# The adaLN products beside the mLSTM of a streaming encoder layer: from full-format matmuls to high and low parts in the rounded format

## The chip, the cores and the metric

The kernel runs as one program on one core of one Trainium2 chip. The metric is the time of one execution on the device, in microseconds (us). One core has five engines that run side by side and wait for each other through semaphores: TensorE (PE in the profile, its weight loads PEld), VectorE (DVE), ScalarE (ACT), GpSimd (POOL) and SyncE (SP), which here only issues DMAs.

## The reference

One layer of a hybrid encoder, for a prompt of 2048 tokens and for a sample of 32 tokens with its states. A conditioning row c gives six rows of shift, scale and gate. The part that the change touches is the product that makes them; the mLSTM is computed at the same time as four of the six.

```python
def adaln(c, w_ada, b_ada):
    mod = jax.nn.silu(c) @ w_ada + b_ada          # (1024) @ (1024, 6144), once for the prompt, once for the sample
    return jnp.split(mod[:, None, :], 6, axis=-1)

def trunk_layer(x, c, p, ...):
    sh1, sc1, g1, sh2, sc2, g2 = adaln(c, p['w_ada'], p['b_ada'])
    h = rmsnorm(x, p['norm1_w']) * (1 + sc1) + sh1
    ... projection; mLSTM in chunks (4 heads of 128); stick-breaking attention ...
    mix = jnp.concatenate([y_a, y_b], axis=-1) @ p['w_out']
    x = x + g1 * mix
    h2 = rmsnorm(x, p['norm2_w']) * (1 + sc2) + sh2
    f_out, conv_new = conv_ffn(h2, conv_state, p['w_up'], p['w_conv'], p['b_conv'], p['w_down'])
    x = x + g2 * f_out
```

## The kernel before

The program has four phases with a barrier of all engines behind each: `front` (the first two adaLN rows, the norm and the combined projection), `attention` (stick-breaking), `mlstm_output` and `ffn`. The change is in `mlstm_output` alone.

`mlstm_output` goes over 17 chunks of 128 tokens, 16 of the prompt and one of the sample. Each engine has its own program in the order in which it is written; nothing is scheduled by a planner. TensorE and VectorE go by slots (`chunks`): slot t works on chunk t and prepares chunk t + 1. TensorE's slot is `turn(t+1)` (the decay exponents into `mpD`, then twelve transposes into `mpT`), `numerator(t)`, `scores(t+1)`, `update(t)` and, last, `modulate(t)`: the product of the activated conditioning (`silu_c`, 128 x 2 for each of eight blocks of the 1024 rows) with 256 columns of `w_ada`, into the PSUM bank `mpm`. There are 16 such products, one in each of the slots 0 to 15. VectorE's slot is `prepare(t+1)` (`mqw`, `mVU`, `mDM` and two copies `mT`), `modulation_row(t-1)` (adds the product to the bias row in `mmod_rows`), `decay(t)` (`mC<-mC,decay`), `weigh(t+1)` (`mSW`) and `finish(t)` (the new memory `mC`, four small operations on `mdn`, and the output tile `mH`). ScalarE scales k (`mks`), copies v (`mVI`), copies a transposed tile (`mT`), takes the exponential (`mWX`), and rounds a piece of the output projection's weights (`w_out_high`). GpSimd issues the DMA that stores `mH`, then subtracts to get the low part of that piece (`w_out_low`).

SyncE issues the loads in the order of the chunks: three tiles `mx`, two small rows, then, when the product two chunks earlier is through with the buffer, 1 MB of `w_ada` into `mwa` (two buffers), and 256 KB of `w_out`. So SyncE waits for a product in each slot and has the next chunk's `mx` queued behind it.

Two number formats matter. A float32 matmul runs as two records for each one that is written; a matmul on tiles of the rounded format (`F32R`, fp32r in the trace) as one. Elsewhere the kernel already works with pairs: a high part, which is the value rounded (ScalarE's copy into an `F32R` tile), and a low part, the value less the high part, with three of the four products of the pairs added up. The mLSTM's own products and the adaLN products are in plain float32.

Behind the last slot come the first two norms of the output stage (`first_norms`, on VectorE), the sample's chunk, and then the output projection, which TensorE carries.

Of the kernel before, what the change touches and what calls it, by code (L numbers as in the profile page):

```python
# [6 lines left out]
F32 = mybir.dt.float32  # L7
# [5 lines left out]
P = 128  # L13
# [1006 lines left out]
def mlstm_output(k, c, gc, dec):  # L1020
# [16 lines left out]
    wo_high, wo_low = k.sems("w_out_high", "w_out_low")  # L1037
    bias_in, mod_psum, mod_ready, mod_turned, mod_row, mod_stored, plus_one, scale_ready = k.sems(
        "bias_loaded", "mod_summed", "mod_ready", "mod_turned", "mod_row_ready", "mod_stored", "scale_plus_one", "scale_ready")
    NM = 6 * KD - NMOD  # L1040
# [11 lines left out]
    with ExitStack() as s:  # L1052
# [11 lines left out]
        with ExitStack() as over:  # L1064
# [9 lines left out]
            yT = psum(nc, over, "eyT", [P, D])  # L1074
        wa = sbuf(nc, s, "mwa", [P, 2, KD, 2 * P])
        mod_rows = sbuf(nc, s, "mmod_rows", [2, NM * P])
# [12 lines left out]
        dn = sbuf(nc, s, "mdn", [P, 4, MH])  # L1089
        H = sbuf(nc, s, "mH", [P, 2, MH, MD])  # L1090
        pT = psum(nc, s, "mpT", [P, 3, W5])
        pN = psum(nc, s, "mpN", [P, 2, W5])
# [34 lines left out]
        def _(sp):  # L1127
# [18 lines left out]
            def body(t, u, r, first):  # L1146
# [9 lines left out]
                if not (isinstance(t, int) and t == NPT):  # L1156
                    if not first:
                        sp.wait_ge(mod_psum, t - 1)
                    sp.dma_start(wa[:, u], d["w_ada"].rearrange("(k p) n -> p k n", p=P)
                                 [:, :, bass.ds(t * 2 * P + NMOD * P, 2 * P)]).then_inc(w_in[u], 16)  # L1160
                    sp.dma_start(wL_plain[:, bass.ds(t, 1)].rearrange("p o n -> p (o n)"),
                                 d["w_out"].rearrange("(k p) n -> k p n", p=P)[bass.ds(r, 1), :, u * W5:(u + 1) * W5]
                                 .rearrange("o p n -> (o p) n")).then_inc(wo_in[u], 16)
# [25 lines left out]
        def _(pool):  # L1189
            nc.gpsimd.memset(LG[:], 1.0).then_inc(ones_ready, 1)  # L1190
            nc.gpsimd.memset(RU[:], 1.0).then_inc(ones_ready, 1)
            nc.gpsimd.memset(VI[:], 1.0).then_inc(ones_ready, 1)
            nc.gpsimd.memset(C[0][:], 0.0).then_inc(ones_ready, 1)

            def body(t, u, r, first):
                pool.wait_ge(h_ready, t + 1)
                pool.dma_start(d["h_d"][tok(t), :], H[:, u].rearrange("p h e -> p (h e)")).then_inc(stored[u], 16)
# [24 lines left out]
        def _(act):  # L1222
# [48 lines left out]
            act.preload_act_table_set("natural_log_exp_and_others")  # L1271
            act.wait_ge(ones_ready, 4)

            def body(t, u, r, first):
# [4 lines left out]
                nc.scalar.activation(ks[:, u], x[:, u, 1], ACT.Copy, scale=MD ** -0.5).then_inc(k_scaled, 1)  # L1279
                nc.scalar.activation(VI[:, u, :, 0:MD], x[:, u, 2], ACT.Copy).then_inc(v_ready, 1)  # L1280
                act.wait_ge(turned, t + 1)
                nc.scalar.activation(T[:, u, 0], pT[:, 0].rearrange("p (h e) -> p h e", e=P), ACT.Copy).then_inc(q_taken, 1)
# [16 lines left out]
        def _(dve):  # L1299
# [124 lines left out]
            def modulation_row(t):  # L1424
                dve.wait_ge(mod_psum, t + 1)
                span = bass.ds(t * 2 * P, 2 * P)
                v.tensor_tensor(mod_rows[:, span], pm[0:2, 0:2 * P], mod_rows[:, span], ALU.add).then_inc(mod_row, 1)

# [22 lines left out]
        def _(pe):  # L1451
# [55 lines left out]
            def modulate(chunk):  # L1507
                t, u, r = chunk
                pe.wait_ge(w_in[u], 16 * r + 16)
                at_least(pe, mod_row, t)  # L1510
                for kk in range(KD):
                    mm = t_.matmul(pm[0:2, 0:2 * P], c["silu_c"][:, kk, :], wa[:, u, kk], start=(kk == 0),
                                   stop=(kk == KD - 1))
                mm.then_inc(mod_psum, 1)

# [674 lines left out]
```

## Time and profile before

| | |
|---|---|
| median of 3 runs | 3301.67 us (3301.16 to 3303.12) |
| the profiled execution's own time | 3299.27 us |
| its span in the profile | 3297.3 us |
| mean granted TensorE clock, share of full speed | 0.983 |
| busy, share of the span | PE 96%, PEld 85%, DVE 47%, ACT 33%, POOL 23% |
| chain that ended last, share of the span | PE 44%, DVE 1%, issue 1% |
| GpSimd's first instruction of `mlstm_output` | 1332.91 us from the span's start |
| TensorE's first matmul of the output projection | 1518.52 us |

The span is the time from the first to the last instruction in the profile; the execution's own time is a little longer. A time in a row counts from the span's start. A busy share says how long an engine had something running, not how long the others waited for it, and the records of TensorE overlap, so that its pace is read from one start to the next.

### The profile page before, as it was taken

The numbers are of one execution on the slowest core, as the hardware profiler recorded it, in microseconds if no ns is written. First come the engines' busy times: TensorE is split into PE (matmuls) and PEld (weight loads), VectorE is DVE, ScalarE is ACT, GpSimd is POOL, SyncE is SP. The second block draws the span as 40 slices with busy tenths as digits, with TensorE's granted clock in tenths as the row PEclk, the third lists the DMA queues.
The fourth block names the chain that finished last, engine by engine and source line by source line (L and its number), as shares of the span: only waits on it lengthen the run. The fifth ranks groups of instructions, "written<-read, shape, count | busy, mean of one in ns | idle before, by whom it ended". The sixth has DMA issues, their size and how long they took to land. (4 is left out here: it accounts for less than half of the span.)

```text
span 3297.3 us, 45305 instructions
## 1 busy us (share of the span) xinstructions
PE 3172.6 (96%) x17258; PEld 2792.8 (85%) x17258; DVE 1539.7 (47%) x1979; ACT 1075.7 (33%) x2073; POOL 773.7 (23%) x688
## 2 busy tenths in 40 slices
PE   7999999898999999899996999999999999999999
PEld 3878887677998999677885999999999998887886
DVE  2300015532898899576652534444444346324331
ACT  3611112222776777224553222212212213213110
POOL 2421113321665666111110111111111115002000
PEclk9999999999999999899997999999999999999999
DMA  5322224433522340575544111111111114444432
GB/s 189 109 72 71 71 71 139 130 109 101 140 53 53 68 87 10 184 249 205 179 150 156 52 51 34 43 51 51 51 48 29 51 51 168 170 144 151 144 120 72
DMA packets 250868, 336.08 MB, mean 102 GB/s; under 512 B 58652, under 2 KB 170840, under 8 KB 243932
## 3 DMA queue, kind: packets, MB, share of 16 engines
q1 hardware_dynamic: 234526, 284.75, 28.3%
q0 software_dynamic: 14864, 49.31, 4.5%
q8 instruction: 94, 1.54, 0.2%
q14 instruction: 52, 0.43, 0.0%
q10 hardware_dynamic: 1332, 0.06, 0.0%
HBM read 225.16 MB, written 108.89 MB: 101 GB/s over the span
## 5 line engine op out<-in xcount | busy, mean ns | idle before, releaser
L2031 PE MATMUL facc<-fh,fwH 128*128 128x416 f32 x3520 | 948.8, 350 | 25.3 <-DVE fh L1916 25.3
L2031 PEld LDWEIGHTS facc<-fh,fwH 128*128 128x128 f32 x3520 | 662.4, 188 | 33.4 <-issue 25.9
L2031 PE MATMUL facc<-fh,fwL 128*128 128x416 f32 x1760 | 622.3, 354 | 0.0
L642 PE MATMUL pacc<-pring,h1H 128*128 128x512 f32 x1360 | 445.0, 398 | 9.5 <-POOL h1L L524 5.8
L952 POOL TENSOR_TENSOR aS<-aS,aC 128x512 f32<-128x512 f32 (+3 forms) x326 | 333.8, 1030 | 191.5 <-DVE aC L914 188.8
L914 DVE TENSOR_TENSOR_SCAN aC<-aB,aC,a 128x512 f32<-128x512 f32 (+3 forms) x326 | 362.7, 1113 | 15.2 <-ACT aB L889 9.0
L1925 DVE TENSOR_SCALAR fV<-fU,fcw,fcb 128x2048 f32<-128x2048 f32 (+2 forms) x90 | 118.4, 1357 | 528.8 <-ACT fU L1799 512.3
L1797 ACT ACTIVATE fU<-facc 128x416 f32<-128x416 f32 (+1 forms) x220 | 112.9, 514 | 771.4 <-PE facc L2031 771.4
L1885 POOL TENSOR_TENSOR fwL<-fraw,fwH 128x1024 fp32r<-128x1024 f32 x44 | 132.7, 3016 | 851.9 <-ACT fwH L1788 851.9
L2031 PEld LDWEIGHTS facc<-fh,fwL 128*128 128x128 f32 x1760 | 330.9, 188 | 2.0
L2057 PE MATMUL dacc<-dfreed 128*128 128x512 f32 (+1 forms) x1380 | 321.4, 390 | 6.4 <-DVE dfreed L1972 3.7
L642 PEld LDWEIGHTS pacc<-pring,h1H 128*128 128x128 f32 x1360 | 259.6, 191 | 65.2 <-POOL h1L L524 5.9
L2057 PEld LDWEIGHTS dacc<-dfreed 128*128 128x128 f32 (+1 forms) x1380 | 248.9, 181 | 72.9 <-POOL dfreed L1898 5.3
L1010 PEld LDWEIGHTS a_out<-av,aA 128*128 128x128 f32 x2176 | 281.7, 191 | 19.1 <-issue 1.9
L1010 PE MATMUL a_out<-av,aA 128*128 128x64 f32 x2176 | 282.8, 269 | 0.0
L642 PE MATMUL pacc<-pring,h1L 128*128 128x512 f32 x680 | 268.2, 394 | 0.0
L968 PE MATMUL a_z<-ak,aq 128*128 128x512 f32 (+3 forms) x640 | 208.4, 408 | 13.1 <-DMA aq<-qk_T 13.1
L889 ACT ACTIVATE aB<-a_z 128x512 f32<-128x512 f32 (+3 forms) x326 | 174.5, 535 | 107.7 <-PE a_z L979 49.3
L642 PE MATMUL pacc<-plate,h1H 128*128 128x512 f32 x544 | 182.2, 395 | 4.9 <-POOL plate L520 4.9
L994 PE MATMUL a_x<-ident,aS 128*128 128x128 f32 x1106 | 176.1, 275 | 4.5 <-DVE aA L881 4.1
L296 ACT ACTIVATE pstage<-pacc 128x512 f32<-128x512 f32 x119 | 70.5, 594 | 323.3 <-PE pacc L642 323.2
L894 ACT ACTIVATE aS<-a_z 128x512 f32<-128x512 f32 (+3 forms) x326 | 174.7, 536 | 0.0
(275 smaller groups left out, 4207.6 us busy)
## 6 DMA issues: line engine op xcount, KB each, us to landing
proj_out<-pstage SPq DMA_DIRECT2D x119, 256.0 KB, 2.0
dfreed_plain<-act_d SPq DMA_DIRECT2D x20, 1408.0 KB, 6.3
fraw<-w_up SPq DMA_DIRECT2D x44, 512.0 KB, 5.5
act_d<-fV SPq DMA_DIRECT2D x21, 1024.0 KB
qk_T<-pturn POOLq DMA_DIRECT2D x68, 256.0 KB, 3.1
mwa<-w_ada SPq DMA_DIRECT2D x16, 1024.0 KB, 5.6
dthird_plain<-act_d SPq DMA_DIRECT2D x11, 1408.0 KB, 6.3
praw<-w_in SPq DMA_DIRECT2D x56, 256.0 KB, 2.8
```

What stands on the lines that cost most here:

```text
L642: op = mm_(acc[:, n % NB], h[:, kk, tok(t)], weight(q, w), start=(kk == 0 and part == 0), stop=(kk == KD - 1 and part == 2))
L889: nc.scalar.activation(part(B, RB, n), part(Z, NZ, n), ACT.Sigmoid, scale=-1.0).then_inc(pass_ready, 1)
L894: nc.scalar.activation(part(S, RS, n), part(Z, NZ, n), ACT.Sigmoid).then_inc(stop_ready, 1)
L914: v.tensor_tensor_scan(buf[:, a:b][:, ::-1], part(B, RB, n)[:, ::-1], nought[:, 0:width(n)], buf[:, b:b + 1], ALU.mult, ALU.add).then_inc( ...
L952: nc.gpsimd.tensor_tensor(at, at, buf[:, a + 1:b + 1], ALU.mult).then_inc(w_ready, 1)
L968: mm = nc.tensor.matmul(to, Q[:, b, half, i * P:(i + 1) * P], K[:, b, span], start=(half == 0), stop=(half == 1), skip_group_check=True)
L994: mm = nc.tensor.transpose(X[:, n % NX, j * P:(j + 1) * P], src[:, j * P:(j + 1) * P], c["ident"][:])
L1010: mm = nc.tensor.matmul(O[:, r % 2, 0:SD if kind == PROMPT else 4 * SD], weight[:, j * P:(j + 1) * P], value, start=(top(n) and j == 0), s ...
L1885: nc.gpsimd.tensor_tensor(wL[:, j], raw[:, j], wH[:, j].bitcast(F32), ALU.subtract).then_inc(w_low, 1)
L1925: v.tensor_scalar(V[:, j, at:at + width], U[:, j, u0:u0 + width], tap(0), cb[:, ft], ALU.mult, ALU.add).then_inc(first_tap, 1)
L2031: mm = nc.tensor.matmul(dst, a[:, j, kk], b[w][:, kk], start=(kk == 0 and m == 0), stop=(kk == KD - 1 and m == 2))
L2057: mm = nc.tensor.matmul(down_acc[0:w, n % 2], at[:, l, kk, 0:w], r, start=(kk == 0 and m == 0), stop=(kk == LAST and m == 2))
```

## The change

Each block of `w_ada` that has landed in `mwa` is split. ScalarE rounds it, half by half (four of eight blocks, 128 x 1024 elements each), into a new tile `mwaH`; GpSimd subtracts that from the raw values and writes the difference over them, in place, as `mwaL`. The conditioning is split once, at the start, into a stationary tile `mcHL` of 34 columns: the high part in columns 0 and 1, zeros in 2 to 31, the low part in 32 and 33. TensorE then makes two matmuls in the rounded format for each of the eight blocks: `mcHL` (34 columns) with `mwaH`, and the first two columns of `mcHL` with `mwaL`. The result stands in rows 0 and 1 and rows 32 and 33 of `mpm`, and VectorE adds both, one after the other, to the bias row. SyncE waits for the product's second half (`mod_half`) where it waited for the product (`mod_psum`).

```diff
@@ buffers and constants
-        wa = sbuf(nc, s, "mwa", [P, 2, KD, 2 * P])
+        with ExitStack() as over:
+            wa = sbuf(nc, over, "mwa", [P, 2, KD, 2 * P])
+        wa_low = sbuf(nc, s, "mwaL", [P, 2, KD, 2 * P], F32R)
+        cHL = sbuf(nc, s, "mcHL", [P, KD, 34], F32R)
+        wa_high = sbuf(nc, s, "mwaH", [P, 2, KD // 2, 2 * P], F32R)
@@ SyncE, body(t)
-                        sp.wait_ge(mod_psum, t - 1)
+                        sp.wait_ge(mod_half, 2 * t - 2)
@@ GpSimd
+            pool.wait_ge(c_set, 2)
+            nc.gpsimd.tensor_tensor(cHL[:, :, 32:34], c["silu_c"][:], cHL[:, :, 0:2].bitcast(F32), ALU.subtract).then_inc(c_set, 1)
+
+            def split_low(t, u):
+                for e in range(2):
+                    half = slice(e * KD // 2, (e + 1) * KD // 2)
+                    pool.wait_ge(wa_split, 2 * t + e + 1)
+                    nc.gpsimd.tensor_tensor(wa_low[:, u, half], wa[:, u, half], wa_high[:, e].bitcast(F32), ALU.subtract
+                                            ).then_inc(wa_done, 1)
 
             def body(t, u, r, first):
+                if not (isinstance(t, int) and t == NPT):
+                    split_low(t, u)
                 pool.wait_ge(h_ready, t + 1)
@@ ScalarE
+            nc.scalar.activation(cHL[:, :, 2:32], C[0][:].rearrange("p h m -> p (h m)")[:, 0:30 * KD]
+                                 .rearrange("p (k j) -> p k j", k=KD), ACT.Copy).then_inc(c_set, 1)
+            nc.scalar.activation(cHL[:, :, 0:2], c["silu_c"][:], ACT.Copy).then_inc(c_set, 1)
+
+            def split_high(t, u, r):
+                act.wait_ge(w_in[u], 16 * r + 16)
+                for e in range(2):
+                    at_least(act, mod_half, 2 * t + e - 1)
+                    at_least(act, wa_done, 2 * t + e - 1)
+                    nc.scalar.activation(wa_high[:, e], wa[:, u, e * KD // 2:(e + 1) * KD // 2], ACT.Copy).then_inc(wa_split, 1)
 
                 nc.scalar.activation(VI[:, u, :, 0:MD], x[:, u, 2], ACT.Copy).then_inc(v_ready, 1)
+                if not (isinstance(t, int) and t == 0):
+                    split_high(t - 1, 1 - u, r - 1 + u)
                 act.wait_ge(turned, t + 1)
@@ VectorE
             def modulation_row(t):
-                dve.wait_ge(mod_psum, t + 1)
+                dve.wait_ge(mod_half, 2 * t + 2)
                 span = bass.ds(t * 2 * P, 2 * P)
-                v.tensor_tensor(mod_rows[:, span], pm[0:2, 0:2 * P], mod_rows[:, span], ALU.add).then_inc(mod_row, 1)
+                v.tensor_tensor(mod_rows[:, span], pm[0:2, 0:2 * P], mod_rows[:, span], ALU.add).then_inc(mod_high, 1)
+                dve.wait_ge(mod_high, t + 1)
+                v.tensor_tensor(mod_rows[:, span], pm[32:34, 0:2 * P], mod_rows[:, span], ALU.add).then_inc(mod_row, 1)
@@ TensorE
             def modulate(chunk):
                 t, u, r = chunk
-                pe.wait_ge(w_in[u], 16 * r + 16)
                 at_least(pe, mod_row, t)
-                for kk in range(KD):
-                    mm = t_.matmul(pm[0:2, 0:2 * P], c["silu_c"][:, kk, :], wa[:, u, kk], start=(kk == 0),
-                                   stop=(kk == KD - 1))
-                mm.then_inc(mod_psum, 1)
+                if isinstance(t, int) and t == 0:
+                    pe.wait_ge(c_set, 3)
+                for e in range(2):
+                    pe.wait_ge(wa_done, 2 * t + e + 1)
+                    for kk in range(KD // 2):
+                        t_.matmul(pm[0:34, 0:2 * P], cHL[:, e * KD // 2 + kk, :], wa_high[:, e, kk], start=(e == 0 and kk == 0),
+                                  stop=False, skip_group_check=True)
+                        mm = t_.matmul(pm[0:2, 0:2 * P], cHL[:, e * KD // 2 + kk, 0:2], wa_low[:, u, e * KD // 2 + kk],
+                                       start=False, stop=(e == 1 and kk == KD // 2 - 1), skip_group_check=True)
+                    mm.then_inc(mod_half, 1)
```

GpSimd's program at its first two chunks, with a minus as it was and with a plus as it is. Names are tiles, `out<-in`; a row is an instruction, x2 two alike.

```order
-L1197 DMA h_d<-mH 128x512
-L1201 TENSOR_TENSOR w_out_low<-w_out_plain,w_out_high 128x512
-L1197 DMA h_d<-mH 128x512
-L1201 TENSOR_TENSOR w_out_low<-w_out_plain,w_out_high 128x512
...
+L1207 TENSOR_TENSOR mwaL<-mwa,mwaH 128x1024 x2
+L1214 DMA h_d<-mH 128x512
+L1218 TENSOR_TENSOR w_out_low<-w_out_plain,w_out_high 128x512
+L1207 TENSOR_TENSOR mwaL<-mwa,mwaH 128x1024 x2
+L1214 DMA h_d<-mH 128x512
+L1218 TENSOR_TENSOR w_out_low<-w_out_plain,w_out_high 128x512
```

Two subtractions of 128 x 1024 stand now ahead of each chunk's store of `mH`, and behind the chunk before's `w_out_low`.

ScalarE's program at the second chunk, as it was:

```order
L1279 ACTIVATE mks<-mx 128x512
L1280 ACTIVATE mVI<-mx 128x4x128
L1282 ACTIVATE mT<-mpT 128x512
L1285 ACTIVATE mWX<-mDM 128x512
L1289 ACTIVATE w_out_high<-w_out_plain 128x512
```

And as it is:

```order
+L1306 ACTIVATE mks<-mx 128x512
+L1307 ACTIVATE mVI<-mx 128x4x128
+L1299 ACTIVATE mwaH<-mwa 128x1024 x2
+L1311 ACTIVATE mT<-mpT 128x512
+L1314 ACTIVATE mWX<-mDM 128x512
+L1318 ACTIVATE w_out_high<-w_out_plain 128x512
```

The two roundings of chunk t - 1's weights stand in chunk t's body, between the copy of v and the copy of the transposed tile for which `scores` waits. TensorE's and VectorE's programs keep their order; only `modulate` and `modulation_row` are longer by the instructions of the diff.

## Rows read from the trace of the kernel before

**Rows 1.** Busy us of PE, PEld, DVE, ACT, POOL; PEclk, DMA share, GB/s.

```profile
1385.00:1395.00 10.00, 9.21 (x66) 6.66 (x65) 7.51 (x15) 2.90 (x5) 1.82 (x2) 1.00 0.75 256
1445.00:1455.00 10.00, 10.00 (x71) 7.32 (x70) 7.96 (x15) 3.17 (x6) 1.82 (x2) 1.00 0.76 257
```

**Rows 2.** TensorE in order of time, one slot; start us, us, engine, line.

```profile
1448.33 1.15 PE L1495 MATMUL mpD<-mRU,mLG 2*128 2x128 f32 x8
...
1454.45 3.62 PE L1512 MATMUL mpm<-mwa,silu_c 128*2 128x256 f32 x16
1457.99 1.15 PE L1495 MATMUL mpD<-mRU,mLG 2*128 2x128 f32 x8
```

**Rows 3.** ScalarE, GpSimd and VectorE in that slot, in order of time.

```profile
1446.40 0.69 DVE L1420 TENSOR_TENSOR mH<-mpN,mdn 128x512 f32<-128x512 f32 x1
...
1447.48 0.63 ACT L1279 ACTIVATE mks<-mx 128x512 f32<-128x512 f32 x1 [1.27 <-DMA mx<-proj_out]
...
1447.75 0.55 POOL L1197 DMA_DIRECT2D h_d<-mH  x1 [7.69 <-DVE mH L1420]
...
1448.31 1.27 POOL L1201 TENSOR_TENSOR w_out_low<-w_out_plain,w_out_high  x1
...
1448.77 1.38 DVE L1375 TENSOR_TENSOR mVU<-mVI,gate_cols 128x516 f32<-128x516 f32 x1 [0.38 <-ACT mVI L1280]
...
1452.87 0.69 DVE L1399 TENSOR_TENSOR mC<-mC,decay 128x516 f32<-128x516 f32 x1 [0.29 <-PE mpN L1542]
...
1455.35 0.16 DVE L1412 SCALAR_TENSOR_TENSOR mdn<-mdn 128x4 f32<-128x4 f32 x1
...
1456.18 0.69 DVE L1420 TENSOR_TENSOR mH<-mpN,mdn 128x512 f32<-128x512 f32 x1
```

**Rows 4.** TensorE in order of time, two products of 512 columns.

```profile
1529.90 0.40 PE L1474 MATMUL eacc<-w_out_high,eyH 128*128 128x512 f32 x1
1530.13 0.40 PE L1474 MATMUL eacc<-w_out_high,eyL 128*128 128x512 f32 x1
```

**Rows 5.** All instructions of three lines: ns min/median/max, first and last start.

```profile
L1885 POOL TENSOR_TENSOR fwL<-fraw,fwH x44: 2329/2767/3395, 1758.3 to 2729.1; 128x1024 fp32r<-128x1024 f32 x44
L524 POOL TENSOR_TENSOR h1L<-h_plain,h1H x17: 2345/2392/2404, 54.5 to 157.9; 128x1024 fp32r<-128x1024 f32 x17
L1788 ACT ACTIVATE fwH<-fraw x44: 1039/1062/1064, 1757.2 to 2727.8; 128x1024 fp32r<-128x1024 f32 x44
```

**Rows 6.** VectorE and GpSimd in the ConvFFN, in order of time.

```profile
1824.98 2.35 DVE L1929 SCALAR_TENSOR_TENSOR fV<-fU,fcw,fV 128x2048 f32<-128x2048 f32 x1
1826.19 3.40 POOL L1885 TENSOR_TENSOR fwL<-fraw,fwH 128x1024 fp32r<-128x1024 f32 x1 [7.89 <-ACT fwH L1788]
1827.24 2.40 DVE L1929 SCALAR_TENSOR_TENSOR fV<-fU,fcw,fV 128x32 f32<-128x32 f32 x1
```

**Rows 7.** First and last slots, in order of time.

```profile
1356.55 3.62 PE L1512 MATMUL mpm<-mwa,silu_c 128*2 128x256 f32 x16
...
1357.45 0.16 DVE L1412 SCALAR_TENSOR_TENSOR mdn<-mdn 128x4 f32<-128x4 f32 x1
...
1358.06 0.69 DVE L1420 TENSOR_TENSOR mH<-mpN,mdn 128x512 f32<-128x512 f32 x1
...
1360.10 1.15 PE L1495 MATMUL mpD<-mRU,mLG 2*128 2x128 f32 x8
...
1504.28 0.69 DVE L1420 TENSOR_TENSOR mH<-mpN,mdn 128x512 f32<-128x512 f32 x1
...
1506.41 0.41 DVE L1427 TENSOR_TENSOR mmod_rows<-mpm,mmod_rows 2x256 f32<-2x256 f32 x1 [1.45 <-PE mpm L1512]
...
1508.07 0.69 DVE L1310 TENSOR_TENSOR ey<-ey,ewrow 128x512 f32<-128x512 f32 x1
```

**Rows 8.** A long wait of TensorE in the projection, and the clock behind it.

```profile
516.73 1.05 PE L683 MATMUL pR<-ident,pstage 128*128 128x128 f32 x4 [2.56 <-DVE pturn L450]
518.00:520.00 2.00, 2.00 (x6) 1.61 (x5) 1.58 (x3) 1.22 (x3) 0.37 (x1) 0.50 0.83 244
```

More of the change, by code:

```diff
@@ L1037, in mlstm_output @@
     wo_high, wo_low = k.sems("w_out_high", "w_out_low")
-    bias_in, mod_psum, mod_ready, mod_turned, mod_row, mod_stored, plus_one, scale_ready = k.sems(
-        "bias_loaded", "mod_summed", "mod_ready", "mod_turned", "mod_row_ready", "mod_stored", "scale_plus_one", "scale_ready")
+    bias_in, mod_ready, mod_turned, mod_row, mod_stored, plus_one, scale_ready = k.sems(
+        "bias_loaded", "mod_ready", "mod_turned", "mod_row_ready", "mod_stored", "scale_plus_one", "scale_ready")
+    wa_split, wa_done, c_set = k.sems("w_ada_high", "w_ada_low", "c_parts_set")
+    mod_half, mod_high = k.sems("mod_half_summed", "mod_high_added")
     NM = 6 * KD - NMOD
```

## The prediction

> **What bounds the kernel now.** I read the page first: TensorE is busy 96% of the span and carries the chain that ended last, so the question is what the changed stage, the mLSTM between 1333 and 1518 us, is worth on that chain. Then the busy times of two stretches [rows 1]: at 1445 TensorE is busy throughout, at full clock, while VectorE has 8.0 of 10 us, ScalarE 3.2, GpSimd 1.8 and the DMA engines 0.76 of their time. The reader is to see that TensorE sets the pace but VectorE is close behind. Then one slot of TensorE in order of time [rows 2]: it starts at 1448.33, the product at 1454.45, the next slot at 1457.99. So a slot is 9.66 us: 6.12 for the chunk, 3.54 for the product, in 16 records of 0.221 us each. From the first whole slot's start at 1360.10 to the last product's reduction at 1506.41 [rows 7] the average is 9.75, since a few slots also wait. Last, what the other engines do in that slot [rows 3]; this decides the case, as follows.
>
> **TensorE's part.** The 16 records become 16 matmuls of 256 columns in the rounded format. No such width of that format is in this stage. Bounds: 512 columns of the same format go by 0.23 us from start to start [rows 4], half of which is 0.115; a record of the old product has 0.221 (no gain at all). The format is the one of rows 4 and only the length differs, so I take 0.115: 1.85 us for 3.54, and a slot that TensorE alone would finish in 7.97. That would be 15 x 1.7, some 26 us, were TensorE the only one to go by.
>
> **ScalarE's part.** Two copies of 128 x 1024 at 1.06 us [rows 5], 2.1 us a slot, beside 3.2 in 10. They need the product before to be through. Behind `mks` (which runs 0.85 us ahead of the slot's start [rows 3]) and the copy of v, they run from about 0.6 to 2.7 us of the slot; behind them waits the copy `mT`, whose transposes end at about 2.4. `scores` needs that copy near 4.1. So ScalarE is covered by some 0.6 us; without the cover each us would be one of the slot.
>
> **GpSimd's part, which I take to be the new bound.** Two subtractions of 128 x 1024. The same shape and formats took 2.33 at least and 2.77 in the median in the ConvFFN, and 2.39 with a spread of 0.06 in the front [rows 5]. The long ones contain waits: the one at 1826.19 took 3.40, but VectorE held it until 1827.3, and from there it is 2.33 [rows 6]. I take 2.39. With the store's 0.55 and the 1.27 of `w_out_low` [rows 3] GpSimd has 6.6 us of work in a slot, which alone would fit.
>
> It doesn't run alone, though. In the slot shown VectorE's `mVU` is given 1.38 us where its neighbours of this shape have 0.69: it starts at 1448.77 inside GpSimd's operation (1448.31 to 1449.58) and ends 0.57 after it [rows 3]. And in the ConvFFN an operation of 32 columns took 2.40, until GpSimd's ended [rows 6]. So VectorE's operations on two SBUF operands wait for GpSimd's subtraction, however small they are, and GpSimd's for theirs. In a slot there are five on VectorE: `mqw`, `mVU`, `decay`, and two small ones on `mdn`. The Trainium skill, in SBUF — State Buffer, section Who interferes with whom, says this: a VectorE instruction with two SBUF inputs and a GpSimd instruction that reads SBUF exclude each other for a whole instruction, and whichever starts first has its way; the trace agrees, with the 1.38 and the 2.40.
>
> Now the loop. GpSimd's order is: store of `mH`, `w_out_low`, first subtraction, second subtraction, then the wait for the next `mH`. VectorE comes to `decay` 4.54 into the slot (1452.87), some 4.7 with the second addition, in the middle of the first subtraction, and gets its turn between the two; its first small operation (7.0 in) falls into the second subtraction and waits for its end; behind it `mH` is queued, and for `mH` GpSimd waits. From one `mH` to the next:
> - end of `mH` (1447.09) to the store 0.66, to `w_out_low` 0.56, its length 1.27 [rows 3];
> - subtraction 2.39; `decay` between them 0.50 (the 0.57 above, less an overlap of 0.07 seen in rows 6); subtraction 2.39;
> - small operations and `mH`: 1.52 from 1455.35 to 1456.87 [rows 3], 1.30 from 1357.45 to 1358.75 [rows 7]; since a blocked operation ends about 0.1 sooner, I take the lower.
>
> That is 9.07 us for 9.75. TensorE's second half of a product starts 0.15 after the second subtraction and takes 0.92, so TensorE waits about 1.1 us between the halves, and its slot ends 0.2 before `mH` does. A rule that speaks against the change is in the GPSIMD Engine Reference of the Trainium skill, section Elementwise — side-by-side cycle accounting: a two-input operation goes at about 2.6 cycles per element. At the page's clock this estimate gives 2.2 us, and a loop of 8.7; the measured 2.39 decides.
>
> **DMA and VectorE beside it.** No transfer is added. SyncE's wait for the product keeps its place: behind it are queued the load of `mwa`, of `w_out` and the next `mx`, which lands about 8.7 us after the slot's start (1457.0 for 1448.33), 0.4 before the next slot at 9.07. So the load stays hidden, at some 0.81 of the DMA engines. The second addition costs VectorE 0.45; it stands ahead of `decay`, which waits for GpSimd anyway: nothing. The three small instructions for `mcHL` run while `mx` loads: nothing.
>
> **The sum**, on the rows of the first and last slots [rows 7]. `mH` of chunk 0 ends at 1358.75, as before. Fifteen loops of 9.07 bring chunk 15's to 1494.8; it was 1504.97. VectorE then starts the last addition at 1494.7 instead of 1506.41: 11.7 us earlier. From there to `ey<-ey,ewrow` it was 1.66. Now 0.45 is added, and `w_out_low` is asked for inside this stretch and holds the port 1.27 us: 2.9, so 1.2 is lost. Behind it everything moves with VectorE. 11.7 - 1.2 = 10.5. One more term: if `decay` comes after the second subtraction has begun, it, `weigh` and the addition to `mC` stand between that one's end and `mH`, and the loop is 1.5 longer, once, since the next starts later. In slot 1 the two are within 0.3 us; at half weight 0.8. Sum 9.7: the profiled execution's own 3299.27 becomes 3289.6, and the median, 2.4 above it, 3292.0.
>
> **Rivals.**
> - *GpSimd's subtractions don't hold up VectorE.* Then VectorE and the transposes make the loop (`mH`'s end 8.54 into the slot, `mqw` 0.6, TensorE ready 1.1 into the next: 8.2, and 0.3 of the second addition): 8.5. 15 x 0.57 and the tail's 1.2 more: 3282. Against it stand rows 3 and 6; for it only that all rows with small operands are of 32 columns, not 4.
> - *The subtraction is longer here*, as in the ConvFFN's median of 2.77: loop 9.83, 11.4 us back: 3303. The same time comes if late `mx` tiles put `mVU` behind `w_out_low` in most slots. Gain and loss meet at 2.74 us.
> - *Slower: TensorE's clock.* TensorE now waits 1.1 us in each slot. At 516.73 it had waited 2.56, and by 518 the granted clock was 0.50, the lower level of 1.2 GHz; at 1385 it waited 0.79 in ten and stayed at 1.00, 2.4 GHz [rows 8, 1]. If 1.1 us is enough, the slot's first 2.4 us take twice as long: 15 x 2.4 = 35, so 3327. It decides somewhere between waits of 0.8 and 2.6. TensorE: Matmul & The Clock Gate (the Trainium skill), What's actually happening, has the same two levels.
> - *The rounded format is no faster at 256 columns*: product 3.54, its second half 1.8 behind the second subtraction, loop about 9.6 to 9.9: 3300 to 3305.
>
> **How the numbers follow.** Forecast (3287 to 3296) 0.50; no hold-up, or a partial one (3280 to 3287), 0.14; longer subtraction, late loads or several slots out of order (3296 to 3308) 0.24; format without gain 0.03; clock, or subtractions of 2.95 and more (over 3308), 0.09. This kernel's measurement can tell about 0.2%, 6.6 us, from no change: faster is below 3295.1, slower above 3308.3. Of the forecast 0.46 of 0.50 lies below 3295.1, so faster 0.60; slower 0.11 with the far part of the longer subtractions; same 0.29. The range leaves out a tenth at either end: 3283 to 3305.
>
> **What the changed profile would show.** The old 256 records' places filled by matmuls with starts 0.11 to 0.12 apart; a wait of about 1.1 us of TensorE for GpSimd's `mwaL` in the middle of each product, at clock 1.00; `mwaL` at 2.3 to 2.5 with `decay` between the two; a small `mdn` operation of about 1 us that ends with the second; slots of 9.0 to 9.2. I am wrong if the small operation isn't held, if the slots are below 8.7, or if the wait of GpSimd isn't for `mH`.

## The result and the profile after

| | before | after |
|---|---|---|
| median | 3301.41 us (3300.24 to 3303.12, 4 runs) | 3324.04 us (3319.04 to 3327.05, 4 runs) |
| ratio of after to before | | 1.0067, 95% interval 1.0049 to 1.0084 |
| profiled execution, its span, mean clock | 3299.27, 3297.3, 0.983 | 3324.46, 3322.8, 0.975 |
| `mH` of chunk 0 to `mH` of chunk 15, end to end | 146.2 us, 9.75 a slot | 169.6 us, 11.31 a slot |

The kernel became slower by 22.6 us, where 3292.0 was forecast. The last row says where: the fifteen slots between those two ends took 23.4 us more. The rest of the span differs by 2 us. (Times of runs below come with the ratio to runs of the kernel before on the same chip; a line number is that of the kernel named.)

The windows that answer to [rows 1], of the changed kernel: busy us of PE, PEld, DVE, ACT, POOL; PEclk, DMA share, GB/s.

```profile
1385.00:1395.00 10.00, 9.87 (x81) 9.16 (x80) 8.22 (x16) 4.16 (x6) 5.20 (x4) 0.94 0.49 153
1445.00:1455.00 10.00, 8.59 (x61) 8.13 (x62) 7.84 (x13) 5.43 (x9) 6.45 (x4) 0.83 0.70 231
```

TensorE was busy throughout at 1445; now it stands idle for 1.4 of 10 us and is at half clock for a third of them. VectorE's busy time has hardly changed (it counts what an operation is held as busy), and GpSimd has 6.45 us. So no engine is full: they wait for each other, and the order in time has to show how. (PEclk is a mean over the window: 0.83 is full clock for two thirds of it and half clock for the rest.) The changed kernel's product first, TensorE in order of time:

```profile
1453.42 0.28 PE L1546 MATMUL mpm<-mwaH,mcHL 128*34 128x256 f32 x1
1453.54 0.28 PE L1548 MATMUL mpm<-mwaL,mcHL 128*2 128x256 f32 x1
1453.65 0.28 PE L1546 MATMUL mpm<-mwaH,mcHL 128*34 128x256 f32 x1
```

Starts are 0.115 us apart, as forecast, only the second comes 0.20 behind the first. From a product's first start to the next slot's it is 2.02 us where TensorE doesn't wait, for 3.54 before; 1.85 was forecast. TensorE's part is right but for those 0.17 us. Now GpSimd and VectorE of the changed kernel in two slots, each engine apart in order of time; they answer to [rows 3].

```profile
1360.60 0.59 POOL L1214 DMA_DIRECT2D h_d<-mH  x1 [5.23 <-DVE mH L1449]
1361.21 1.28 POOL L1218 TENSOR_TENSOR w_out_low<-w_out_plain,w_out_high 128x512 fp32r<-128x512 f32 x1
1362.44 4.64 POOL L1207 TENSOR_TENSOR mwaL<-mwa,mwaH 128x1024 fp32r<-128x1024 f32 x2
...
1391.58 4.67 POOL L1207 TENSOR_TENSOR mwaL<-mwa,mwaH 128x1024 fp32r<-128x1024 f32 x2
...
1360.82 6.83 DVE L1404 TENSOR_TENSOR mVU<-mVI,gate_cols 128x516 f32<-128x516 f32 x1
...
1393.29 3.53 DVE L1428 TENSOR_TENSOR mC<-mC,decay 128x516 f32<-128x516 f32 x1
1396.84 0.69 DVE L1416 TENSOR_TENSOR mSW<-mpS,mWX 128x512 f32<-128x512 f32 x1
```

The two subtractions take 4.64 and 4.67 together, 2.33 each, with nothing between them. `decay` comes at 1393.29, in the middle of the first, and ends at 1396.82, 0.57 behind the second: it was not let in between. In the other slot `mVU` comes at 1360.82, while GpSimd issues its DMA, and is held for 6.83 us: through that, `w_out_low` and both subtractions, to 0.57 behind the last. Over the stage:

```profile
L1428 DVE TENSOR_TENSOR mC<-mC,decay x15: 672/1905/3526, 1370.1 to 1523.7; 128x516 f32<-128x516 f32 x15
```

That is the group of all 15 `decay` of the prompt's chunks from the second on: ns least, median, most, against 0.69 in [rows 3]. Five of them take 3.48 to 3.53, as the one above. Six take 1.8 to 2.2: they are issued only when the second subtraction runs, like this one (GpSimd, then VectorE).

```profile
1448.06 4.66 POOL L1207 TENSOR_TENSOR mwaL<-mwa,mwaH 128x1024 fp32r<-128x1024 f32 x2
...
1451.48 1.80 DVE L1428 TENSOR_TENSOR mC<-mC,decay 128x516 f32<-128x516 f32 x1 [1.41 <-PE mpN L1578]
```

All eleven end some 0.57 behind the second subtraction. The other four take 0.67 to 0.70; three of them are in the slots with a long `mVU`. `mVU` is held 6.78 to 6.83 us three times. From one `mH` to the next it is 10.4 to 10.6 us in the eleven slots with a held `decay`, once 11.07, and 14.3, 14.5 and 13.8 in the three with the long `mVU`.

### The profile page after: what moved, and what is told of

It reads as the page before. It is cut to its first block and busy times, and to the rows that moved or that the text cites. A ratio compares the mean times of both kernels' runs of the same rounds, so it can differ in the third digit from the quotient of the medians.

```text
span 3322.8 us, 45499 instructions
## 1 busy us (share of the span) xinstructions
PE 3170.1 (95%) x17258; PEld 2817.6 (85%) x17258; DVE 1573.4 (47%) x1995; ACT 1107.3 (33%) x2107; POOL 847.4 (26%) x721
```

## The experiments

"Spacing" is the mean from one end of `mH` to the next, chunk 0 to 15; it is read in each profile in the way of the last row of the table above.

| kernel | median, us | ratio to before (95%) | spacing |
|---|---|---|---|
| `old_product_split_beside` | 3325.37 | 1.0067 (1.0045 to 1.0089) | 11.59 |
| `turns` | 3308.04 | 1.0020 (1.0009 to 1.0030) | 10.15 |
| `turn_for_decay` | 3319.00 | 1.0051 (1.0035 to 1.0066) | 10.87 |
| `free_of_port` | 3309.39 | 1.0025 (1.0015 to 1.0035) | 10.49 |
| `store_by_sync` | 3324.70 | 1.0062 (1.0047 to 1.0077) | 10.92 |
| `own_waits` | 3305.84 | 1.0008 (0.9999 to 1.0018) | 9.87 |
| `no_low` | 3299.82 | 0.9994 (0.9984 to 1.0003) | 9.75 |
| `no_low_early_loads` | 3277.84 | 0.9929 (0.9912 to 0.9946) | 8.31 |
| `before_early_loads` | 3299.19 | 0.9994 (0.9984 to 1.0004) | 9.66 |
| `own_waits_early_loads` | 3299.83 | 1.0001 (0.9991 to 1.0010) | 9.53 |
| `turns_early_loads` | 3298.06 | 0.9991 (0.9982 to 1.0001) | 9.75 |
| `turns_early_store` | 3321.84 | 1.0058 (1.0041 to 1.0074) | 10.42 |
| `all_handed_over` | 3283.35 | 0.9939 (0.9926 to 0.9953) | 8.15 |
| `before_same_moves` | 3307.57 | 1.0019 (1.0010 to 1.0028) | 9.66 |
| `handed_store_by_gpsimd` | 3281.88 | 0.9937 (0.9921 to 0.9952) | 8.46 |
| `handed_late_loads` | 3300.19 | 0.9992 (0.9983 to 1.0002) | 9.60 |
| `handed_over_tail` | 3279.91 | 0.9926 (0.9913 to 0.9940) | 8.12 |

**Is it the product, or what prepares it?** `old_product_split_beside` keeps the kernel before and its product, and adds only the roundings and the subtractions, whose results nobody uses:

```diff
+                if not (isinstance(t, int) and t == 0):
+                    split_high(t - 1, 1 - u, r - 1 + u)
...
+                if not (isinstance(t, int) and t == NPT):
+                    split_low(t, u)
```

> The kernel before, with its float32 product, and beside it ScalarE's roundings and GpSimd's subtractions, whose results nothing uses. Theory P: the loop from mH to mH is the one of the changed kernel, 10.5 us or more, time 3318 to 3328. Theory C: the product in two float32 passes keeps TensorE busy and its clock near 1.00, so the time is within 5 us of 3301.

It loses the same as the changed kernel, though its clock falls less: over the stage, 1360 to 1530 us, the mean granted clock is 0.95 in its profile and 0.88 in the changed kernel's. So the loss comes from the work beside TensorE, and neither from the new matmuls nor from a clock that would fall because they are short.

**Is it the port?** `turns` makes GpSimd wait for the two held operations:

```diff
                 for e in range(2):
                     half = slice(e * KD // 2, (e + 1) * KD // 2)
                     pool.wait_ge(wa_split, 2 * t + e + 1)
+                    pool.wait_ge(vw_ready if e == 0 else decayed, t + 2 - e)
```

> GpSimd's first subtraction of a block waits until VectorE's mVU is done and its second until VectorE's decay is done; nothing else is changed. Theory P (port kept): GpSimd keeps the shared port over operations that it has queued, so decay waits for both subtractions (3.48 us in the changed kernel) and mVU now and then for three operations (6.8 us). Then this kernel hands the port over: decay about 1 to 2 us at most, loop from mH to mH 9.1 to 9.4 for 10.6, time 3293 to 3300. Theory C (clock): TensorE's waits pull its clock to about 0.85 and that makes the slots long. TensorE still waits in the middle of each product here, so the time stays at 3312 to 3325.

16 us of the 22.6 come back, below the range of the clock theory, but above the 3293 to 3300 that I expected of the other. No `decay` takes over 1.07 us, no `mVU` over 2.25. Only the shorter slots reach 9.2, and between them stand others of 10 to 13.4.

`turn_for_decay` keeps the second of these waits alone (`if e == 1: pool.wait_ge(decayed, t + 1)`).

> The changed kernel with one wait more: GpSimd's second subtraction waits for decay (the computation is whole). It makes the order that my forecast took for granted (decay between the two subtractions). Port theory: decay is 0.7 to 1.1 us and not 3.5, the slots that were 10.54 become 9.1 to 9.3, but mVU is held as before (where GpSimd's DMA issue or w_out_low runs, 3 us and more), so the time is between turns and the changed kernel, 3308 to 3316 us. Rival, all of the loss is in mVU: 3322 to 3326 us as the changed kernel.

`decay` is down to 1.2 us at most, but `mVU` is now held for 4.0 to 4.6 us seven times, and slots alternate between 9.1 and 12.3. It gave back 5 us and not the 8 to 16 that I expected: in this order, most of the price passes to `mVU`.

`free_of_port` takes the port away from VectorE: ScalarE does `decay`, four copies with a scale, and the denominators are two operations that read PSUM.

```diff
-                v.tensor_copy(dn[:, 0].rearrange("p (b h) -> p b h", b=2), num[:, :, :, MD]).then_inc(dn_ready, 1)
...
+                v.scalar_tensor_tensor(out=pair(dn[:, 1]), in0=num[:, :, :, MD], scalar=-1.0, in1=pair(g[:, 2]), op0=ALU.mult,
+                                       op1=ALU.max).then_inc(ab_ready, 1)
...
+                v.tensor_tensor(pair(dn[:, 2]), num[:, :, :, MD], pair(dn[:, 1]), ALU.max).then_inc(fl_ready, 1)
@@ ScalarE, behind the exponential
...
+                    for h in range(MH):
+                        op = nc.scalar.activation(C[0][:, h], C[0][:, h], ACT.Copy,
+                                                  scale=dec[:, bass.ds(t - 1, 1), h:h + 1].rearrange("p o h -> p (o h)"))
+                    op.then_inc(decayed, 1)
```

> The changed kernel with decay of chunks 0 to 15 on ScalarE (four copies with a scale, behind mWX) and the denominators from PSUM in two VectorE operations with one SBUF operand each instead of three, so that of VectorE's operations only mqw and mVU can meet GpSimd at the port. Theory P: loop 8.3 to 8.9, except where mVU is caught; time 3282 to 3291. Theory C: no difference to the changed kernel beyond the shorter chain on VectorE, 3312 to 3322.

Slots of 7.9 appear, the length that TensorE alone would need, but beside 12.0, and three `mVU` of 6.8 with slots of 14 to 14.7. So the 3309.39 misses the 3282 to 3291 that I expected.

**By what rule does GpSimd keep the port?** `store_by_sync` gives the store of `mH` to SyncE (`sp.dma_start(d["h_d"]...)` behind `w_out`'s load, none on GpSimd).

> The changed kernel with only the store of mH issued by SyncE in place of GpSimd (the computation is whole). If the hold-ups of 6.8 us of mVU come about because it is issued while GpSimd's DMA issue runs and GpSimd's next three operations follow at once, they are gone or different: the three slots of 13.8 to 14.5 us shrink to about 10.6, and the time is 3310 to 3316 us. Rival, w_out_low alone holds mVU as long: no change, 3321 to 3327 us.

The time is unchanged, for two reasons that cancel. The holds of 6.8 us are gone, as expected, but eleven `mVU` of 2.84 to 2.86 took their place, and the fifteen slots took 5.8 us less in all; and from chunk 15's `mH` to the end of the span it is 7.2 us longer, which comes back below. The profile showed something else too: VectorE's `mVU` and GpSimd's pair of subtractions.

```profile
1409.10 2.85 DVE L1410 TENSOR_TENSOR mVU<-mVI,gate_cols 128x516 f32<-128x516 f32 x1
...
1408.50 5.67 POOL L1215 TENSOR_TENSOR mwaL<-mwa,mwaH 128x1024 fp32r<-128x1024 f32 x2 [4.99 <-ACT mwaH L1305]
```

Here `mVU` ends at 1411.95, inside the pair, and the pair takes 5.67 and not 4.67: VectorE was let in between. What differs is ScalarE's second rounding: here it ended at 1409.37, after the first subtraction had begun (1408.50), so that the second still had a wait unmet at that time; in the changed kernel both roundings were over at 1361.32, before the first subtraction (1362.44). `own_waits` tests just that, with waits of GpSimd for itself:

```diff
                     pool.wait_ge(wa_split, 2 * t + e + 1)
+                    at_least(pool, wo_low if e == 0 else wa_done, t if e == 0 else 2 * t + 1)
```

> The changed kernel, its computation whole, with two waits of GpSimd for itself and for nothing else: before the second subtraction it waits until its own first one is through, and before the first until its own last w_out_low is. No order between engines is set. Theory 1, GpSimd goes on with the port when its next operation has nothing left to wait for at the time it comes up, and gives it to a waiting VectorE when it has to stop for a semaphore (in store_by_sync mVU was let in after the first subtraction, 2.85 us, where the rounding of the second half ended while the first subtraction ran; in the changed kernel both roundings were through before): decay is held for one subtraction at most (1 to 2.4 us), no mVU over 2.5, loops of 9.1 to 9.4 where the loads are in time, 3304 to 3313 us, near turns. Theory 2, GpSimd has the port until its queue is empty or it waits for another engine: decay 3.5 and mVU 6.8 stay, 3320 to 3327 us.

No order between engines is set, and still 18 us come back. No `mVU` is over 2.24 and no `decay` over 2.35, one operation of GpSimd at most beside a DMA issue; pairs take 4.85 to 5.83 us. So it is the queue: GpSimd goes straight on to its next operation when that has nothing left to wait for early enough, and VectorE, though it waited first, comes behind all of them. How early is not settled. In `store_by_sync` the second rounding ended 0.87 us after the first subtraction had begun, and VectorE was let in, eleven times of eleven. In `old_product_split_beside` roundings ended 0.37 to 0.77 after the operation before had begun, in two slots, and `mVU` was held through all the same; here ScalarE, GpSimd and VectorE in one of them:

```profile
1400.65 1.99 ACT L1290 ACTIVATE mwaH<-mwa 128x1024 fp32r<-128x1024 f32 x2
...
1402.27 4.65 POOL L1202 TENSOR_TENSOR mwaH<-mwa,mwaH 128x1024 fp32r<-128x1024 f32 x2
...
1400.88 6.61 DVE L1396 TENSOR_TENSOR mVU<-mVI,gate_cols 128x516 f32<-128x516 f32 x1 [0.38 <-ACT mVI L1298]
```

The Trainium skill, in SBUF — State Buffer, section Who interferes with whom, has it that the port pair shared by VectorE and GpSimd is an exclusive lock, and that the order of issue decides who blocks. The trace agrees for one instruction; over several it doesn't hold, since in the changed kernel the second subtraction starts some 0.6 us after `decay` was issued, and ahead of it. The measurement decides.

**And the load of `mx`?** `no_low` drops GpSimd's subtractions altogether; the second matmul of a pair reads the high part again, so the low part of the weights is missing from its result.

> Leaves out GpSimd's subtractions: the second matmul of each pair reads the high part again, so TensorE's and ScalarE's work is that of the changed kernel but the low part of the weights is not in the result. Theory P: the whole loss and more is the subtractions'; the loop is VectorE's, 8.3 to 8.7 us, time 3280 to 3286. Theory C: some waits of TensorE stay, for VectorE, and the clock stays below 0.95 in this stage; 3290 to 3305. A third, theory A (ScalarE's two roundings ahead of mT delay scores): 3300 or more.

A miss for the port theory, and the most useful one: without the subtractions there is no gain either. The time lies in the range of theory C, and the mean clock over the stage, 0.94, fits it too, so it takes a further run to tell. In the profile of `no_low`, SyncE, then TensorE, ScalarE, VectorE and GpSimd, in order of time:

```profile
1441.38 0.39 SPq L1165 DMA_DIRECT2D mwa<-w_ada  x1
1441.99 0.40 SPq L1167 DMA_DIRECT2D w_out_plain<-w_out  x1
1442.67 1.52 SPq L1158 DMA_DIRECT2D mx<-proj_out  x3
...
1441.12 1.15 PE L1523 MATMUL mpD<-mRU,mLG 2*128 2x128 f32 x8
...
1450.61 1.15 PE L1523 MATMUL mpD<-mRU,mLG 2*128 2x128 f32 x8 [1.29 <-DMA mRU<-ug_d]
1452.87 1.09 PE L1532 MATMUL mpT<-ident,mx 128*128 128x128 f32 x4 [1.12 <-issue]
1453.76 1.06 PE L1532 MATMUL mpT<-ident,mqw 128*128 128x128 f32 x4
...
1450.65 0.63 ACT L1303 ACTIVATE mks<-mx 128x512 f32<-128x512 f32 x1 [1.50 <-DMA mx<-proj_out]
...
1450.88 1.90 DVE L1399 TENSOR_TENSOR mqw<-mx,gate_cols 128x512 f32<-128x512 f32 x1 [1.16 <-DMA mx<-proj_out]
...
1450.93 1.28 POOL L1216 TENSOR_TENSOR w_out_low<-w_out_plain,w_out_high  x1
```

The slot begins at 1441.12. The loads of the next chunk are issued from 1442.67 on and end their waits at 1450.6, 9.5 into the slot; TensorE waited 1.29 for `mRU` and 1.12 more behind `mqw`, which came late enough to meet `w_out_low` and took 1.90 for 0.68; TensorE then has its transposes at 0.85 to 0.89 us a group of four, where 0.44 is the pace at full clock. The windows say the same (clock 1.00, then 0.83):

```profile
1440.00:1450.00 10.00, 9.20 (x79) 8.10 (x76) 8.42 (x21) 4.80 (x7) 1.83 (x2) 1.00 0.70 236
1450.00:1460.00 10.00, 8.28 (x57) 8.01 (x58) 6.90 (x10) 5.00 (x8) 1.83 (x2) 0.83 0.71 237
```

So most slots alternate: 8.0, late load, fallen clock, 12.2; after the long one the load is in time again. `no_low_early_loads` moves the issue of `mx`, `mLG` and `mRU` for the chunk after ahead of SyncE's wait for the product:

```diff
             def body(t, u, r, first):
+                if isinstance(t, int) and t == 0:
+                    load_x(0, 0, True)
+                elif not (isinstance(t, int) and t == NPT):
+                    load_x(t + 1, 1 - u, False)
                 if not (isinstance(t, int) and t == NPT):
                     if not first:
                         sp.wait_ge(mod_half, 2 * t - 2)
```

> As no_low (GpSimd's subtractions are left out and the second product of each pair reads the high part again, so the modulation rows lack their low parts), and SyncE now issues the loads of mx, mLG and mRU for the chunk after next before it waits for the product, where they stood behind mwa and w_out_plain. Late-loads theory: without subtractions the slots alternated 8.0 and 12.2 us because the loads are issued 1.5 us into a slot and land some 6.5 us later, which is after the end of a slot of 8.0, and TensorE's clock falls in the wait that follows; with the loads earlier every slot is 8.0 to 8.5, the stage is 16 x 1.6 shorter than in no_low, 3273 to 3283 us. Rival, the loads are late only because something else is (GpSimd's queue, the clock): the 12s stay and the time is that of no_low, 3297 to 3302.

Confirmed: 22 us, by a move of five DMA issues. With the loads in time no `mqw` is over 0.69 and the clock is 1.00 over the stage, so these 22 us are the wait, the held `mqw` and the fallen clock together, and the clock fell with the late load and not without it. `before_early_loads` is the control on the kernel before.

> The kernel before with only that move of the loads. In its slots of 9.66 us TensorE waits for nothing, so the loads are in time: no change, 3299 to 3303 us, by either theory. Should it be faster by over 3 us, then the kernel before loses time to late loads too and the gain of the runs beside it is not the gain of the product.

No change there, as both theories said. So the load had room in slots of 9.66 and none in slots of 8.

**Both steps put right.** `own_waits_early_loads` is the changed kernel as my forecast described it.

> own_waits with the early loads (the computation is whole): the changed kernel as my forecast described it, with decay let in between the two subtractions and the load of mx hidden. If these two steps are all that failed, slots of 9.1 to 9.3 us and 3289 to 3297 us, where the forecast had 3292; else, with something more missing, 3298 us and more.

One slot of it, TensorE, VectorE and GpSimd apart in order of time:

```profile
1453.94 0.31 PE L1555 MATMUL mpm<-mwaH,mcHL 128*34 128x256 f32 x1 [0.91 <-POOL mwaL L1216]
1455.00 1.15 PE L1535 MATMUL mpD<-mRU,mLG 2*128 2x128 f32 x8
...
1450.55 1.10 DVE L1437 TENSOR_TENSOR mC<-mC,decay 128x516 f32<-128x516 f32 x1
...
1453.08 0.83 DVE L1450 SCALAR_TENSOR_TENSOR mdn<-mdn 128x4 f32<-128x4 f32 x1
...
1448.74 5.15 POOL L1216 TENSOR_TENSOR mwaL<-mwa,mwaH 128x1024 fp32r<-128x1024 f32 x2
```

`decay` is let in between, the small operation on `mdn` is held to the second subtraction's end, and TensorE waits 0.9 to 1.15 between the halves. Eleven of the fifteen slots are 8.95 to 9.32, where I had 9.07. But one is 9.52, and three are 11.0 to 11.3, and the time, 3299.83, is outside the 3289 to 3297 that I expected. In those three the clock is down (busy us of PE, PEld, DVE, ACT, POOL; PEclk, DMA share, GB/s):

```profile
1407.00:1409.00 2.00, 2.00 (x10) 2.00 (x11) 0.86 (x2) 0.00 (x0) 1.84 (x3) 0.50 0.82 230
...
1457.00:1459.00 2.00, 2.00 (x20) 2.00 (x19) 1.42 (x4) 1.12 (x2) 1.86 (x2) 1.00 1.01 325
```

Before 1407 TensorE had waited 1.15 us in the product, and before 1457 it had waited 0.91: half clock, 1.2 GHz, in the one and full clock, 2.4 GHz, in the other. But 1.15 us before the slot at 1445.92 had no such effect, so the length of one wait doesn't decide, and that the wait pulls the clock down isn't shown by a run of its own. These three slots are a third missing term of some 6 us, and no gain is left: ratio 1.0001.

`turns_early_loads` has the waits of `turns` and the early loads.

> As turns (the two subtractions of GpSimd wait for mVU and for decay, the whole computation is done) with the early loads. In turns the slots were 9.2 alternating with 10.0 to 13.4. Late-loads theory: the short ones stay at 9.2 and the long ones come to it, 16 x 9.3 instead of 16 x 10.2, 3290 to 3297 us. Rival, the long slots come from mVU held 1.75 us behind the split of w_out: they stay, 3304 to 3308.

Five slots of its fifteen are 10.1 to 12.0 us; the time is 1 us above the range I gave. `turns_early_store` adds the store on SyncE and lets `w_out_low` wait for `decay` too.

> As turns_early_loads, and the store of mH is issued by SyncE instead of GpSimd, and the split of w_out on GpSimd waits for decay like the second subtraction, so nothing of GpSimd stands at the start of a slot when mqw and mVU run. If GpSimd's DMA issue and the 1.28 us of w_out_low there held mVU (1.75 us in turns), mVU is 0.69 in every slot, slots are 8.6 to 9.2, the time 3284 to 3292 us. Rival, mVU's hold-up was off the path: the time of turns_early_loads within 2 us.

A clear miss. `mVU` is 0.69 in every slot, but behind `decay` GpSimd now has the second subtraction and `w_out_low` in one run, and the small operations on `mdn` wait twice: 0.82 and 1.21 us in one slot, both 128 x 4. The slots become 9.6, and seven of fifteen 10.9 to 12.7. An order that helps one operation gives the wait to the next. Against `turns_early_loads` that is 10 us in the fifteen slots; another 11 lie behind chunk 15's `mH`, at the end that `store_by_sync` has too.

**Nothing left to exclude.** `all_handed_over` has `free_of_port`, the early loads, the store on SyncE, and `pool.wait_ge(vw_ready, t + 2)` before the first subtraction.

> The changed kernel, its computation whole, with four things together: the early loads; the store of mH issued by SyncE; decay on ScalarE and the denominators in two VectorE operations that read PSUM; the first subtraction of GpSimd waits for mVU. The only VectorE operations with two inputs in SBUF are then mqw and mVU, at the start of a slot, while GpSimd waits. Theory (the port and the loads are all that stood between the product and its gain): slots of 8.1 to 8.6 us as in no_low_early_loads, 3276 to 3286 us, below both kernels. Rival: ScalarE's four decays (1.26 us a slot) or the second subtraction's end bind the slot, 9.2 us, 3293 to 3299 us.

Eleven of the fifteen slots are 7.9 to 8.1 us, the longest 9.0, and it beats both kernels by 0.6% and more. `before_same_moves` has the moves of loads, store, decay and denominators on the kernel before.

> The kernel before (product in f32, no split of w_ada) with the same moves of loads, store, decay and denominators, to tell their own worth from that of the rounded product. TensorE's work of 9.66 us a slot sets its slots, so no change: 3299 to 3303 us. Rival: the moves themselves shorten the slot, then it is faster by more than 3 us.

Its spacing is 9.66, so the moves don't shorten a slot. It is slower by 0.2%, above the range I gave, and in its profile the stretch behind chunk 15's `mH` is 8 us longer. Between it and `all_handed_over` lie 24 us, and 15 x 1.5 = 23 is what the rounded product saves TensorE: the gain is the product's. That end is the next thing: in both kernels, and in `store_by_sync` and `turns_early_store`, the last `mH` comes 17.7 to 18.0 us behind the one before it, against 10.7, since SyncE issues the next stage's loads behind a store that waits. `handed_over_tail` puts them ahead of it.

> all_handed_over with one thing more: after the last slot SyncE issues the loads of the next stage before the store of the last but one mH, not behind it (the computation is whole). In all_handed_over those loads left at 1484.65 behind a store that waited for mH, and the last chunk's mH ended 17.95 us after the one before it, against 10.7 in the kernel before. If that wait cost what it looks like, the last interval falls to 11 or 12 us and the time to 3275 to 3280 us; rival, the next stage has slack there: 3282 to 3285 us as all_handed_over.

The last interval is 11.65 us, and 3.4 us of the 6 came back in the median; the intervals of the two ratios overlap, so that part of the gain isn't clear of noise. Its windows answer to [rows 1] too:

```profile
1385.00:1395.00 10.00, 9.98 (x88) 9.20 (x87) 7.46 (x16) 7.13 (x15) 6.90 (x4) 1.00 0.88 294
1445.00:1455.00 10.00, 10.00 (x85) 8.87 (x83) 7.91 (x16) 7.81 (x15) 6.28 (x4) 1.00 0.83 280
```

TensorE is full again, now with shorter slots. Last, what each move is worth. `handed_store_by_gpsimd` leaves the store on GpSimd:

> all_handed_over with the store of mH back on GpSimd (the computation is whole, the order at the end is the old one). Theory that GpSimd's DMA issue and the split of w_out behind it hold mqw or mVU by about 1 to 2 us: slots of 8.0 to 8.8, 3278 to 3288 us. Rival: a hold there is so long that the slots go over 9.2 and the time is above 3293 us.

`mVU` is held 2.0 to 2.2 us in seven slots, and the spacing is 8.46, yet the time is that of `all_handed_over`, since its end is the old one. And `handed_late_loads` differs from this kernel in the place of the loads alone:

> handed_store_by_gpsimd with the loads of mx, mLG and mRU back where the changed kernel has them, behind SyncE's wait for the product and behind mwa and w_out_plain (the computation is whole). Late-loads theory: with the port free the slot wants 8 us and the loads are late again, slots alternate 8 and 12, 3298 to 3304 us, some 16 us or more above the kernel beside it. Rival: the load's lateness mattered only together with the port's hold-ups: within 4 us of the kernel beside it.

18 us between them: the late load costs that much by itself, in a kernel that does the whole computation.

## Why the prediction was wrong

- **The order of the work, TensorE's product, the subtraction's own length: right, or nearly.** 0.115 us from start to start, 2.02 a product for my 1.85; a subtraction of 2.33 to 2.38 for my 2.39.
- **The step that failed first: "`decay` ... gets its turn between the two".** I took the ConvFFN's alternation [rows 6] for a rule. There 43 of the 44 subtractions of GpSimd had waited for ScalarE; here both roundings were through before the first subtraction, and GpSimd went on without a stop. I had priced the other order, "the loop is 1.5 longer, once", at half weight 0.8. It was not once: eleven slots had it, 9.07 + 1.5 = 10.57, and 10.40 to 10.64 were measured; over fifteen slots that is 22.5 us for my 0.8. It alone puts the loop above the old 9.75. In five of the eleven `decay` was issued in the first subtraction and held through both; in six it came only when the second ran, behind waits and a fallen clock of TensorE. Both kinds of slot are equally long.
- **The same step, `mVU`.** I had "late `mx` tiles put `mVU` behind `w_out_low`" as a rival of 3303, at 1.3 us a time. It is put behind `w_out_low` and both subtractions: (14.31 + 14.46 + 13.80) - 3 x 10.57 = 10.9 us in three slots. With the loops, 15 x (10.57 - 9.75) = 12.3, that is 23.2 of the 23.4 us that the stage lost.
- **The second failed step: "so the load stays hidden".** I had it land 8.7 us into the slot, 0.4 before a slot of 9.07. I find no sign that it set the changed kernel's time, though no run has that kernel with the early loads alone; but `own_waits` against `own_waits_early_loads` is 6 us, and at 8 us a slot it is 18 to 22.
- **The rival on the clock: right in kind, in part; its 3327 is close to 3324.04 by luck.** With both steps put right, three slots in fifteen lose some 2 us each; but it isn't decided by the length of one wait, as I had it, since 1.15 us went both ways. In the changed kernel the clock fell too, to 0.83 at 1445, but there `decay` waits for GpSimd in any case: the six slots with a fallen clock and a late `decay` have 10.40 to 10.64, the five others 10.44 to 10.58. And `old_product_split_beside` loses as much with its product at the old pace.
- **The loop itself: right where its premises held.** 9.07 was forecast, and eleven slots of `own_waits_early_loads` have 8.95 to 9.32.
- **The gain of TensorE's shorter slot, "some 26 us, were TensorE the only one to go by": right.** `no_low_early_loads` and `handed_over_tail` have 23 and 22 us, as 15 x 1.5 would give with the product at 2.02.
- **Slips in my numbers, none of which moved the forecast:** from 1827.33 the operation of [rows 6] runs 2.26 us and not 2.33; the loop without a hold-up adds up to 8.04 before the second addition, not 8.2; and gain and loss meet at 2.39 + 9.7 / 30 = 2.71, not 2.74.

What stays open: why the clock is down behind one wait of 1.15 us and not behind another; how early a wait of GpSimd must be met for it to go straight on; and why a VectorE operation that is issued within GpSimd's DMA issue already has to wait. The profiles show where that begins. Of the `mqw` and `mVU` issued in this stage while GpSimd issued the store of `mH`, all that came 0.17 us or more into that issue were held (49, over thirteen of these kernels and the one before; the three long ones above came at 0.21 to 0.24), and none that came within 0.15 (nine). No run tests it by itself.

## What to carry to other kernels

Before giving work to GpSimd beside VectorE, list VectorE's operations with two SBUF inputs and look at GpSimd's queue behind each: operations with nothing to wait for go as one block, so a hold is as long as the block and not as one operation. A wait of GpSimd for its own last operation breaks the block cheaply; taking VectorE off the port (an input in PSUM, ScalarE) does away with it. And when a slot is to become shorter, work out anew every load that was just in time, for it will be the next bound.

## What the hardware showed that I had not expected

- GpSimd's next operations went ahead of a VectorE operation that already waited for the port: 3.5 us for `decay` (two subtractions), 6.8 for `mVU` (DMA issue and three). With a wait of GpSimd for its own operation before, as in `own_waits`, VectorE was let in: 2.35 and 2.24 at most.
- Operations of 128 x 4 elements are held like large ones: 0.83 and 1.22 us for 0.16.
- Behind waits of about 1 us in TensorE the granted clock was at half in some slots and full in others: slots of 11.0 and 9.2 in `own_waits_early_loads` both had a wait of 1.15 us before them. Where TensorE had no such waits, in `no_low_early_loads` and `handed_over_tail`, it was 1.00 over the stage.
